# One line of dense work per block, with pairs of heads as 64-row score tiles, in a chunked-attention and short-convolution encoder layer

## The reference, cut to what matters

```python
x = layer_norm(x, ln0_g, ln0_b)
proj = x @ w_in                        # 1024 -> 8 groups of 512 columns
q, k, v, z_a, bg, cg, h, z_c = split(proj, 8)
# 8 heads of 64; a chunk of 64 queries sees itself and the 8 chunks before it (576 keys)
s = einsum('bqhd,bkhd->bhqk', qb, kb) / 8 + bias[rel]     # learned, clipped relative position
y_att = softmax(s) @ vb * silu(z_a)
u = cg * h                             # causal depthwise convolution of 3 taps, per channel
y_conv = bg * (conv_b + sum(conv_w[i] * u shifted by 2 - i)) * silu(z_c)
h = concat([y_att, y_conv]) @ w_out
out = layer_norm(ALPHA * x + h, ln_g, ln_b)               # ALPHA = 2 ** 0.25
```

## Time and profile before

| what | before |
|---|---|
| median of 3 runs (lowest to highest) | 1482.03 us (1480.97 to 1482.16) |
| the profiled execution | 1480.33 us, span of its slowest core 1478.8 us |
| spans of the eight cores | 1471.5 to 1478.8 us |
| PE, DVE, ACT, POOL busy | 93%, 73%, 44%, 20% of the span |
| granted clock of TensorE, mean of the cores | 0.985 to 0.988 |
| transfers | 117 MB, 79 GB/s on average |

### The profile page before, as it was taken

How to read it: one execution, slowest core, us unless ns; L and a number is a source line. 1 busy time by engine, 2 the same in 40 slices (tenths; PEclk the granted TensorE clock), 3 DMA queues, 4 the chain that set the end, 5 groups by cost and what they waited for, 6 DMA issues and landing times.

```text
span 1478.8 us, 28799 instructions; the slowest of 8 cores (1471.5 to 1478.8 us)
## 1 busy us (share of the span) xinstructions
PE 1382.6 (93%) x8896; PEld 705.1 (48%) x8896; DVE 1080.5 (73%) x1810; ACT 656.2 (44%) x1189; POOL 295.9 (20%) x629
## 2 busy tenths in 40 slices
PE   4888999999998999999998999999999899999994
PEld 2433545545444554545544454454544445454551
DVE  4488868869586786868869686786868868686657
ACT  4432544535344363544533355353543435355350
POOL 4543202112020221202111020221202112020201
PEclk9999999999999999999999999999999999999997
DMA  8963313213131230313213131220313212141101
GB/s 263 303 161 101 113 29 116 42 46 90 25 121 37 78 74 22 113 31 102 52 48 90 26 122 37 78 74 22 113 32 115 43 56 82 22 123 37 58 8 65
DMA packets 125428, 117.23 MB, mean 79 GB/s; under 512 B 103136, under 2 KB 103136, under 8 KB 125152
## 3 DMA queue, kind: packets, MB, share of 16 engines
q1 hardware_dynamic: 125280, 115.40, 27.6%
HBM read 57.69 MB, written 33.55 MB: 62 GB/s over the span
## 4 chain that ended last, share of the span: by engine, by line
PE 68%; DVE 15%; issue 8%; DMA 3%; POOL 2%; ACT 2%; SPq 0%; DVEq 0%; ACTq 0%; POOLq 0%
PE mm L486 29%; PE mm L767 15%; PE mm L499 13%; PE sc L643 5%; PE pv L677 3%; DVE stats L384 3%; PE sc L650 3%; DVE xs L437 2%; ACT PT L656 2%; DVE ynorm L686 1%; POOL w_in_sb L364 1%; DMA stg<-w_in 1%; DVE acc L604 1%; DVE acc L608 1%; DVE tz L582 1%
## 5 line engine op out<-in xcount | busy, mean ns | idle before, releaser
L486 PE MATMUL mm<-xnT,w_in_sb 128*128 128x512 bf16 x3072 | 768.0, 380 | 41.2 <-DVE tz L582 33.8
L656 ACT ACTIVATE PT<-sc 128x384 bf16<-128x384 f32 (+1 forms) x672 | 342.8, 526 | 407.2 <-PE sc L643 190.6
L486 PEld LDWEIGHTS mm<-xnT,w_in_sb 128*128 128x128 bf16 x3072 | 288.4, 98 | 297.3 <-issue 53.9
L499 PE MATMUL mm<-w_in_sb,xnT 128*128 128x512 bf16 x1024 | 253.1, 379 | 1.0 <-POOL w_in_sb L364 1.0
L643 PE MATMUL sc<-qz,kT 128*128 128x512 bf16 (+3 forms) x896 | 238.5, 300 | 5.7 <-ACT PT L656 4.1
L767 PE MATMUL mm<-w_out_sb,yT 128*128 128x512 bf16 x1024 | 231.0, 387 | 10.0 <-POOL w_out_sb L364 4.6
L677 PEld LDWEIGHTS pv<-vA,PT 128*128 128x128 bf16 x2240 | 160.8, 98 | 160.8 <-issue 8.5
L677 PE MATMUL pv<-vA,PT 128*128 128x65 bf16 x2240 | 183.2, 194 | 3.5 <-ACT PT L656 3.5
L772 DVE TENSOR_TENSOR xs<-xs,mm 128x512 f32<-128x512 f32 x128 | 87.9, 687 | 130.7 <-PE mm L767 129.9
L767 PEld LDWEIGHTS mm<-w_out_sb,yT 128*128 128x128 bf16 x1024 | 101.4, 99 | 136.6 <-issue 20.5
L650 PE MATMUL sc<-etab,ident 128*128 128x256 bf16 (+1 forms) x608 | 154.1, 254 | 0.0
(11 more groups left out here) (61 smaller groups left out, 1189.5 us busy)
## 6 DMA issues: line engine op xcount, KB each, us to landing
xs<-x SPq DMA_DIRECT2D x64, 512.0 KB, 4.6
out<-xs SPq DMA_DIRECT2D x64, 512.0 KB, 5.3
g1bc_sb<-w_in SPq DMA_DIRECT2D x7, 512.0 KB, 8.3
b1bc_sb<-w_in SPq DMA_DIRECT2D x7, 512.0 KB, 8.4
xs<-w_in SPq DMA_DIRECT2D x6, 512.0 KB, 10.3
stg<-w_in SPq DMA_DIRECT2D x6, 512.0 KB, 8.4
vA<-w_in SPq DMA_DIRECT2D x6, 512.0 KB, 8.1
yT<-ytok SPq DMA_TRANSPOSE x128, 2.3
```

Source lines behind the costliest of these rows:

```text
L486: P.op("pe", lambda e, i=i, kc=kc: e.matmul(mm[i][:, :], lhsT=w_in_sb[:, kc, c0:c0 + 128], rhs=xnT[:, sl, kc, :], start=(kc == 0), stop=(k ...
L499: P.op("pe", lambda e, i=i, kc=kc, t=t, c0=c0: e.matmul(mm[i][:, :], lhsT=xnT[:, sl, kc, t * 128:(t + 1) * 128], rhs=w_in_sb[:, kc, c0:c0 ...
L656: P.op("act", lambda e, i=i, coff=coff, hb=hb, j0=j0: e.activation(out=PT[:, hb, OFF[j0]:OFF[j0] + coff], in_=sc[i][:, 0:coff], func=AF.Ex ...
```

## The change

All 40 dense units of a block stand in one line (`block`, `run_units`). Block b's line holds its own values and convolution, the output units of block b-1 and the query, key and gate units of block b+1. In a middle block the order is: 2 value units, 4 output units, 2 value, 4 output, three channel groups of the convolution (12), queries and keys of head pairs 0 and 1 (4), the fourth channel group (4), pair 2 (2), the gate (4), pair 3 (2). Other work is laid along this line at positions counted in dense matmuls: 12 score batches at equal distances S (26.7 dense matmuls), PV of a pair at 0.42, 0.82 and 1.35 S after its last batch, LayerNorm steps at written-out unit numbers.

Heads go in pairs. `qT` holds the queries of two heads in its two halves of 64 rows without zeros; a score matmul contracts over the 64 rows of one head, and the two heads of a pair write two different PSUM banks of one tile `sc`. The bias table is cut into key halves, so a key tile has four bias matmuls of 64 rows where two heads had two of 128. One ACT instruction takes both heads' exponents (`PT[:, :, ...]`). `pv` is one PSUM bank for two token tiles and a pair, where there were two banks.

In both LayerNorms the mean is subtracted from `mv` directly (no `nmean`), and in all but the last tiles the second pass, `x * rstd + beta`, runs on POOL as a multiplication and an addition of 1024 elements each (`affine`). The first convolution tap moves from DVE to ACT, the halo copies from DVE to POOL, the other taps follow their unit at 4, 8 and 12 dense matmuls. `xs` has 10 slots in place of 8, `gate` is held twice, the staging buffer `stg` is gone and the weights of the gate (group 3) come before those of the values (group 2).

```diff
-NSLOT = 8
+NSLOT = 10
-    qz = sb("qz", [128, 4, 2, NTB], BF16)
+    qT = sb("qT", [128, 4, NTB], BF16)
-    sc = [ps("sc%d" % i, [128, 512], F32) for i in range(NSC)]
-    pv = [ps("pv%d" % i, [128, TPB, 65], F32) for i in range(2)]
+    sc = [ps("sc%d" % i, [128, 2, 512], F32) for i in range(2)]
+    pv = ps("pv", [128, 2, 2, 65], F32)
...
+    def affine(s, rs, tab, xres, rd, eng):
+
+        if eng == "dve":
+            P.op("dve", lambda e: e.scalar_tensor_tensor(
+                out=xs[:, s, :], in0=xs[:, s, :], scalar=rs, in1=tab[:], op0=ALU.mult, op1=ALU.add),
+                reads=xres + rd, writes=xres)
+        else:
+            P.op("pool", lambda e: e.tensor_scalar(
+                out=xs[:, s, :], in0=xs[:, s, :], scalar1=rs, scalar2=None, op0=ALU.mult),
+                reads=xres + rd, writes=xres)
+            P.op("pool", lambda e: e.tensor_tensor(
+                out=xs[:, s, :], in0=xs[:, s, :], in1=tab[:], op=ALU.add),
+                reads=xres + rd, writes=xres)
...
+                for hh in range(2):
+                    P.op("pe", lambda e, x=x, n=n, coff=coff, ks=ks, kt=kt, hh=hh, j=j, nob=nob: e.matmul(
+                        sc[x][:, hh, coff:coff + n],
+                        lhsT=kT[64 * hh:64 * hh + 64, ks, pair, kt * 128:(kt + 1) * 128],
+                        rhs=qT[64 * hh:64 * hh + 64, pair, LO[j] * 64:(HI[j] + 1) * 64], start=True, stop=nob),
+                        reads=["kT%d_%d" % (ks, pair), "qT%d" % pair], writes=["sc%d" % x])
+                if not nob:
...
+                    for hf in range(2):
+                        for hh in range(2):
+                            P.op("pe", lambda e, x=x, hh=hh, hf=hf, a0=a0, nn=nn, c0=c0: e.matmul(
+                                sc[x][:, hh, a0:a0 + nn], lhsT=identR[64 * hh:64 * hh + 64, hf, :],
+                                rhs=etab[64 * hh:64 * hh + 64, pair, hf, c0:c0 + nn],
+                                start=False, stop=(hf == 1)),
+                                reads=["identR", "etab"], writes=["sc%d" % x])
...
+        if b:
+            units += conv[0] + conv[1] + conv[2] + qk[0] + qk[1] + conv[3] + qk[2] + za + qk[3]
...
+        S = 8 * nu / 12.0
+        base[0] = pos_now[0]
+        for s in range(12):
+            at(s * S, lambda s=s: qk_batch(b, s // 3, s % 3, has_prev))
+        for p in range(4):
+            z = (3 * p + 2) * S
+            at(z + 0.42 * S, lambda p=p: pvq.append(pv_stage(b, p, (0, 1), 0, has_prev)))
+            at(z + 0.82 * S, lambda p=p: pvq.append(pv_stage(b, p, (2,), None, has_prev)))
+            at(z + 1.35 * S, lambda p=p: pvq.append(pv_stage(b, p, (3,), 1, has_prev)))
```

More of the change, by code:

```diff
@@ L617, in unit_h @@
[L617 to L629 removed]
+             reads=[ur, "mm%d" % i], writes=[ur])
+        P.op("act", lambda e: e.activation(
+            out=acc[:], in_=ubuf[:, cc % 2, 2:NTB + 2], func=AF.Identity, scale=cwh[:, 8 + cc:9 + cc],
+            bias=cbh[:, cc:cc + 1]),
+            reads=[ur, "cw"], writes=["acc"])
```

617 lines of the change are left out of this document (295 added, 322 removed).

## The result

The changed kernel takes **1770.84 us** (median of 4 runs, 1770.12 to 1773.83), where the kernel before takes 1482.1 us: a ratio of 1.194 with a 95% interval of 1.189 to 1.198, 19% slower. The prediction, 1421 us with a range to 1483, was wrong, and on the wrong side.

The account below looks back on a forecast made before the run. PE bounds the kernel, with DVE able to stop it. 1480.3 - 59.4 (scores) + 29 (switches) - 17.3 (waits) - 7 (start) - 6 (end) = 1419.6 us, so a median of 1421 us, range 1370 to 1483.

Parts of the forecast that it names:

- The pairs overlap: Score matmuls on PE: a pair's two 64-row matmuls stream side by side, -59.4 us over all blocks.
- the switch: PE's 352 changes between 128-row and 64-row matmuls: 29 us in all, half of the 58 us upper end.
- DVE's work: VectorE's busy time in a middle block: falls from 66.4 to 52.5 us.
- The sum's terms: Whole kernel, against 1480.3 us: scores -59.4, switches +29, block waits -17.3, start -7, end -6 us.
- 2.5 us per block: PE's waits in blocks 2 to 15: 1.5 us in the first 12 units, 1 us elsewhere; -17.3 us in all.
- With all bounds at once: Whole kernel's time with every term at its bound: given as 1361 to 1495 us.
- The pair 2.1 to 3.1 us.: GpSimd's multiplication and addition for one second pass: 2.1 to 3.1 us, at most 25 us per block added.
- POOL is far from full, and the clears of `PT` ... have more than one S.: GpSimd's queue: it has room, and clears behind a pair have over 6 us until PV reads them.
- the first 12 units: A block's first 12 of 40 units: VectorE and PE each have some 24.6 us of work.
- I take 7 off: Start of the kernel: 7 us less of 25 us of waits, bounds -14 to +3.
- The rival on the other side: First 12 units: DVE and POOL hold each other up, at 2 us per pair 1561 us; chance 0.09.

Follow-up runs that it names:

- e5: The changed kernel with both LayerNorms' second passes left out wherever GpSimd did them, so the output is unscaled: 1475.69 us, 0.996 of the kernel before.
- e14: e5 with early weight casts, block 0's residual passes late and longer time for PV's evacuation: 1429.20 us, 0.963 of the kernel before.
- e2: The changed kernel with halo copies moved to VectorE and PT clears to ScalarE, LayerNorm passes still on GpSimd: 1753.74 us, 1.186 of the kernel before.
- e1: The changed kernel with all second LayerNorm passes back on VectorE: 1681.84 us, 1.137 of the kernel before.
- e9: e1 with about half of the LayerNorm passes moved to where VectorE has room, late in a block: 1588.26 us, 1.069 of the kernel before.
- e7: e1 with a pair's PV spread out to give its evacuation longer time: 1627.66 us, 1.099 of the kernel before.
- e12: e10 with second passes 7 or 8 dense matmuls behind the first, PT clears on ScalarE, block 0's entry LayerNorm spread: 1488.37 us.
- e10: e9 plus the edits of e7 and e6, with block 0's passes moved: 1550.46 us, 1.046 of the kernel before.
- e6: e1 with block 0's weight casts issued ahead: 1658.32 us, 1.120 of the kernel before.
- e16: e12 with all second passes on GpSimd, one to two units more before their results are needed, halo copies on VectorE: 1543.66 us, 1.036 of the kernel before.

## Why the prediction was wrong

The miss is 350 us, 1770.84 against 1421. The forecast had the second passes cost nothing on PE's path; without them 295 us go (e5). The early casts, block 0's moved passes and PV's longer time take 46 more (e14), and then 8 are left.

**What held.** The pairs overlap, the switch cost what the sum had, and DVE's work fell to 55.63 us (forecast 52.5). The sum's terms give a full block of 86.4 - 4.24 + 24 x 0.083 + 2.5 = 86.7 us; without the second passes it lasts 86.2 us (median, e5). So the "2.5 us per block" of waits was about right for the DVE that it was worked out for. The changed kernel's block is 19 us longer than the sum, and that came through POOL. ("With all bounds at once" should read about 1363 to 1500 us; the result lies outside of that too.)

**"The pair 2.1 to 3.1 us."** The first step that failed: 5.4 us. I priced a multiplication like a cast of the same size, 1.04 us, and it takes 2.9 to 3.0. For the addition a price was to be had: the Trainium skill, GPSIMD Engine Reference, section Elementwise — side-by-side cycle accounting, gives 4497 ns for 2048 float32 elements, so half of it, 2.25 us, as an estimate; the trace agrees (2.38 to 2.55 us).

**"POOL is far from full, and the clears of `PT` ... have more than one S."** It failed together with the price. With eight pairs POOL is only 54% busy in a block, but they come in a row. A share says nothing of a queue: what counts is the longest row of work that can stand before the clear, the halo copy and the scaling, and three pairs are 20 us, where one S is some 6. That ACT waits for POOL's result and DVE for its copy was in no step, and the first matters: with the clears and copies out of the queue only 17 us come back, and the scaling still waits (e2). Together these steps cost nearly all of the 295 us of e5. Moving the passes to VectorE gives back only 89 (e1), because there they cost 206 in this order.

**What VectorE would have cost** was no term, since the plan had no second passes on it, but it decides how to mend the kernel. With all passes on VectorE a middle block is 14.3 us longer than without them (99.94 and 85.65). The prediction had the first 12 units break even on paper, without these passes. DVE then has gaps too, waits for the inverse deviation between two passes, and the late evacuation at the one `pv` bank, each of which PE pays. Better places, more time for PV and the order of e12 gave 94 (e9), 54 (e7, alone) and 62 us (e12, after e10).

**The clock** had no term. In the changed kernel's block it is 0.92 of full, and PE is busy for 89.17 us in it, 5 more than without the passes (84.10). In e1's block it is 0.95; in e12's, where PE waits about 1 us at a time (29.5 us in 30 waits for the output's additions), it is 1.00. That the clock falls because of the waits is read from rows; no run separates the two.

**The start, "I take 7 off".** Of the wrong sign: e6 gives back 23.5 us with the casts ahead of need. On the slowest cores block 1's output starts at 214.2 us before the change, at 254.1 in e5 and at 228.2 in e14, and the line has six more units, some 10 us, ahead of it: 29 us late, and 4 us with the start mended. The look-ahead that the old heads had (`need_w` of a later group at each head) was dropped with them, and I read its removal as nothing.

**The rival on the other side**, that DVE and POOL hold each other up, is not what happened: in the changed kernel DVE's 55.63 us in a block are 1.6 more than without the passes. Over 16 blocks that is 26 us of the 295, if PE paid for all of it. In e16 it is real: 62.20 against 54.02 us, 8 us per block, of which 3.4 are the halo copies; of the rest, the product into `yT` takes 1.16 us for 0.70, and the gate's product after PV 0.65 for 0.43 (means of e16 and e5).

What stays open: how the 295 us divide between the clear, the copy and the scaling, how the 41 us of e12 without the clears divide between the gap and the statistics' new places, and how e16's 77 us divide between longer passes on VectorE, the late loads and the start.

## What to carry to other kernels

Before work goes to an idle engine, look at what already stands in its queue and who waits for it: price the longest row of new work ahead of each small urgent instruction and of each result that another engine needs, not the engine's share. When stages are melted into one line, add up every engine's work over short stretches and put what has slack into the stretch where that engine idles; here the same work in another order was worth most of 193 us (e1 to e12; 21 of them are the clears, which went to another engine). A look-ahead that was attached to a loop goes with the loop.
